# Row jobs first, taps as sums and differences, and two pieces of work moved across stage borders

## The chip, the core and the metric

One Trainium2 chip, one core. The kernel is one program in which every engine has a list of instructions of its own: TensorE (PE in the profile), VectorE (DVE), ScalarE (ACT), GpSimd (POOL) and SyncE (SP). Engines wait for one another with counted semaphores. The metric is device time in microseconds. All arithmetic is 32-bit float; one matmul call of the program stands in the trace as two MATMUL records, a transposition as one.

## The reference, cut to what matters

Two layers over 1024 latent and 128 context tokens of width 1024. Each layer mixes tokens and then runs a routed mixture of 16 experts.

```python
hs = rms_norm(xs, norm1_g[l]) * (1.0 + sc1s) + sh1s        # the same for the context tokens
# layer 0 (even):
proj = hs @ w_in                                            # hyena input 1536 | q | k | v | g, 512 each
h = (sin_features @ f3w).reshape(L, 2, 2, 512) * window     # two filters, each forward and backward
h = h / (sum(abs(h), axis=(0, 2)) + EPS)
kern = concatenate([fwd, 0, bwd[1:][::-1]])                 # per filter
z = long_conv(v, kern[0], hbias[0]) * x1                    # v, x1, x2 from the hyena input
y_hy = long_conv(z, kern[1], hbias[1]) * x2
y_ret = silu(g) * head_group_norm(retention(q, k, v))       # chunks of 128, forward and backward
y = concatenate([y_hy, y_ret]) @ w_out
# layer 1 (odd): q, k, v = split(hs @ w_in, 3); rotary on q and k; differential attention; output projection
xs = xs + gate * y                                          # then norm, router, top-k, experts, residual
```

Outputs: both token sets after a final norm, the context's retention state, and its keys and values.

## The kernel before, in words

**Tiles and weights.** The 1152 tokens are nine tiles of 128 (0 to 7 latent, 8 context). Every weight matrix is cut into units of 2 MB (1024 rows by 512 columns, or tables of that size). SP loads units in one fixed order into `ring`, which has four slots; a unit is loaded when the unit four before it has been given back. Four big tensors hold everything else and are reused by each stage: `big`, `hT`, `yT`, `misc`. Each stage names views of them. PSUM (`ps`) has eight banks of 512 columns.

**The order of work** is written out by hand for each engine. The stages are: start (filters of the convolution, and modulation vectors from 24 weight units), normalization `n10`, the combined projection of the even layer, retention, convolution, output projection, normalization `n20`, experts; then `n11`, the projection of the odd layer, attention, output projection, `n21`, experts.

**Start.** A list `start_plan` mixes three kinds of step on PE, ACT and DVE. A *tap* step makes 512 filter columns for a tile of positions and one direction: PE multiplies `f3w` by the features, DVE multiplies by the window into `FH` (L1667), ACT takes the absolute value (L1330), DVE adds it to `facc`. After both directions of a tile, DVE makes their sum and difference into `FS`. There are 18 tap steps per filter, with a modulation unit after every third. A *sum* step adds up `facc` across partitions on PE (L810); DVE adds EPS (L1679) and inverts. Then *dft* steps transform `FS`, and POOL writes the spectra to memory.

**Normalization.** POOL loads the tiles of X. For three tiles at a time ACT squares and sums each tile (L1353), DVE and ACT make the inverse root, and DVE scales the tiles into `XN` (L1725). PE turns each tile (eight 128 by 128 transpositions, L838); ACT writes four of the turned blocks to `hT` with scale and shift (L1346) and DVE the other four. All nine tiles are turned before the first projection matmul.

**Projection.** A *T job* (column job, L856) computes 128 output columns for all tokens, transposed: 8 steps in depth times 3 groups of 384 tokens, 48 records. An *N job* (row job, L859) computes 512 columns for one tile of tokens: 16 records. Jobs alternate between two groups of three banks; ACT evacuates each, and job j waits for the evacuation of job j - 2. The even layer runs 8 T jobs (q, k), 18 N jobs (v, g) and 12 T jobs (hyena); the hyena columns go through a short convolution on DVE and out to memory (`ud`). The odd layer runs 16 T jobs (q, k) and 18 N jobs (v).

**Retention to convolution.** After the last chunk product on PE (L914), `r.o` lets POOL load `ud` back into `zT` (two loads of four pieces). PE turns the gated retention result of nine tiles into the upper half of `yT` (the depth blocks 4 to 7 of the output projection). The convolution has eight items: item i is filter i // 4, channel block i % 4. For an item PE turns the piece (`turn`, L949), ACT copies it to `vt` (L1418), PE transforms it (`forward`, L966, 64 records, and two products for the context), ACT copies the upper half of the spectrum and the context part, DVE reads the spectrum out of PSUM (L1889, L1890), DVE and POOL multiply with the filter, PE transforms back (`back`, L992), ACT copies (L1439), and DVE forms bias and gate. POOL starts each item with six short operations for the context and goes on with four main ones. PE runs two items ahead: `turn` and `forward` of i + 2 stand before `back` of i.

**Output projection.** PE first spreads the gate over partitions (32 records, L1022), which ACT copies into `grow`. Then 18 jobs of 16 records (tile and half, L1034) use four banks in turn, and DVE adds gate times result to X.

Of the kernel before, what the change touches and what calls it, by code (L numbers as in the profile page):

```python
# [17 lines left out]
ALU = mybir.AluOpType  # L18
# [6 lines left out]
P = 128  # L25
# [84 lines left out]
def build(nc, a, out, tab):  # L110

    with ExitStack() as ctx:
        def sb(name, shape, dt=F32):
# [11 lines left out]
                "o.g": 1, "o.gev": 4, "o.mm": 2 * T, "o.x": 2 * T, "o.x_out": 16 * 8, "o.xn_out": 16 * 8,  # L125
# [14 lines left out]
                   "a.ckT": ("r.ktev", T), "a.tev": ("r.oev", T), "a.e": ("h.vtev", 24), "h.xt": ("f.h3", 36), "h.cx": ("f.abs", 36), "h.cs": ("f.acc", 36),  # L140
                   "h.Y": ("f.taps", 36), "h.uw": ("f.dftmm", 18), "h.yc": ("f.sum", 2), "h.xh": ("f.fold", 2),
                   "h.cxev": ("p.u", 12), "h.ycev": ("f.arg", 2), "h.yev": ("f.sin", 2),
# [74 lines left out]
        even_units = w_units(a["w_in_even"][0], [1536, 2048, 2560, 3072, 0, 512, 1024])  # L217
# [15 lines left out]
        odd_units = w_units(a["w_in_odd"][0], range(0, 3072, 512))  # L233
# [22 lines left out]
        FH = big[:, 0:9216].rearrange("p (t d c) -> p t d c", t=T, d=2)  # L256
# [13 lines left out]
        ftmp = big[:, 5120:7168].rearrange("p (f c) -> p f c", f=4)  # L270
        f3w = misc[0:64, :]
        habs = [big[:, 9216 + 512 * i:9728 + 512 * i] for i in range(2)]
# [4 lines left out]
        vtok = big[:, 9216:13824].rearrange("p (t c) -> p t c", t=T)  # L277
        gtok = big[:, 13824:18432].rearrange("p (t c) -> p t c", t=T)
# [19 lines left out]
        vt = big[:, 13824:18432].rearrange("p (b n) -> p b n", b=4)  # L298
# [78 lines left out]
        for o in range(2):  # L377
# [12 lines left out]
        even_jobs = ([(even_units[0], "T", c) for c in range(4)] + [(even_units[1], "T", c) for c in range(4)]  # L390
                     + [(even_units[2], "N", t) for t in range(T)] + [(even_units[3], "N", t) for t in range(T)]
                     + [(even_units[4 + c // 4], "T", c % 4) for c in range(12)])
        odd_jobs = ([(odd_units[c // 4], "T", c % 4) for c in range(16)]
                    + [(odd_units[4 + u], "N", t) for u in range(2) for t in range(T)])
# [102 lines left out]
        def _(pool):  # L497
# [19 lines left out]
            for o in range(2):  # L517
                if o == 1:

                    pool.wait_ge(*at("f.fold", 2))  # L520
                    load_x(a["x_sample"][0], a["x_prompt"][0], (8, 7))
# [9 lines left out]
                if o == 1:  # L531
                    load_x(a["x_sample"][0], a["x_prompt"][0], (6, 5, 0, 1, 2, 3))
# [25 lines left out]
            for i in range(2):  # L558
                ld(zT[i], ud[4 * i:4 * i + 4].rearrange("c p t -> p c t"), f"h.u{i}")
            ld(kctx, kcd, "h.kctx")  # L560

            def hyena():
# [3 lines left out]
                for i in range(8):  # L566
# [16 lines left out]
                    pool.wait_ge(*at("h.cs", i + 1))  # L583
                    if i < 7:
# [157 lines left out]
        def _(pe):  # L742
# [47 lines left out]
            for kind, o, j in start_plan:  # L790
                if kind == "sine":
                    sine_layer(o)
                elif kind == "tap":
                    if j == 0 and o == 0:
                        pe.wait_ge(*at("f.sin", 2))
                    if j >= 4 or o:
                        pe.wait_ge(*at("f.taps", max(18 * o + j - 3, 18 * o)))
# [9 lines left out]
                elif kind == "sum":  # L807
                    pe.wait_ge(*at("f.acc", 18 * (o + 1)))
# [36 lines left out]
            def project(p, jobs):  # L845

                for j, (n, kind, c) in enumerate(jobs):
                    landed(pe, n)
                    if j >= 2:
                        pe.wait_ge(*at(p + "ev", j - 1))  # L850
                    b = 3 * (j % 2)
                    w = slot(n).rearrange("p (k n) -> p k n", k=DK)
                    for k in range(DK):
                        if kind == "T":
                            for g in range(3):
                                i = mm(ps[:, b + g, 0:384], w[:, k, c * P:(c + 1) * P],  # L856
                                       hTv[:, k, g * 384:(g + 1) * 384], start=k == 0, stop=k == DK - 1)
                        else:
                            i = mm(ps[:, b, :], hTv[:, k, c * P:(c + 1) * P], w[:, k, :],  # L859
                                   start=k == 0, stop=k == DK - 1)  # L860
                    i.then_inc(s(p + "mm"), 1)
                pe.wait_ge(*at(p + "ev", len(jobs)))

            def retention():
# [31 lines left out]
                for c in range(T):  # L896
# [32 lines left out]
            def hyena():  # L929

                def turn(i):

                    c = i % 4
                    if i < 4:
                        pe.wait_ge(*at("h.u0", 16))
                    else:
                        pe.wait_ge(*at("h.z", i - 3))
                    for u, tiles in enumerate((range(4), range(4, 8), (8,))):
                        if u < 2 and i:
                            pe.wait_ge(*at(("h.ycev", "h.cxev")[u], (max(i - 2, 0), i)[u]))  # L940
                        if u == 2:
                            pe.wait_ge(*at("h.vtev", 3 * i + 1))
                        for m in tiles:
                            if m < 8:
                                t0 = 512 * (m % 2) + m // 2
# [6 lines left out]
                def forward(i):  # L952
# [6 lines left out]
                    if i:  # L959
                        pe.wait_ge(*at("h.xt", i))  # L960
# [1231 lines left out]
```

## Time and profile before

| what | us |
|---|---|
| median of three runs | 3970.93 (3963.55 to 3975.09) |
| the profiled execution | 3972.35 |
| its span | 3970.4 |
| PE busy with matmuls | 3659.8 (92%) |
| PE busy with weight loads (beside matmuls) | 2883.8 (73%) |
| DVE busy | 1724.4 (43%) |
| ACT busy | 800.1 (20%) |
| POOL busy | 412.3 (10%) |

The mean granted clock of PE is 0.957 of full speed. Shares are averages over stages: experts, projections and attention are dense on PE, and the stages between them are not. Where a row has a count (x8), it stands for so many records that follow one another, the first number is the start of the first, the second their busy time together. A row at the edge of a stretch counts only what lies inside it. "PEclk" is the granted clock as a part of 2.4 GHz: 0.50 is 1.2 GHz.

### The profile page before, as it was taken

To read this page: it belongs to the slowest core of one execution; us is meant where nothing else is said; L and a number is where in the kernel's file an instruction comes from. 1 tells how busy PE (TensorE), PEld (TensorE's weight loads), DVE (VectorE), ACT (ScalarE), POOL (GpSimd) and SP (SyncE) were. 2 spreads that over 40 slices of the span, in tenths; PEclk is the share of its full clock that TensorE was granted. 3 is DMA by queue.
4 is the path that set the end of the run, shared out by engine and by line. 5 is a ranking of instruction groups with operands and counts; after the bars stand their busy time and mean duration, and the time that the engine had idled before them with its cause. 6 is when DMAs were issued, how large, how long until landed. Compare 5 with 4: busy or idle time off the path is not lost. (4 is left out here: it accounts for less than half of the span.)

```text
span 3970.4 us, 53619 instructions
## 1 busy us (share of the span) xinstructions
PE 3659.8 (92%) x22408; PEld 2883.8 (73%) x22408; DVE 1724.4 (43%) x4132; ACT 800.1 (20%) x1878; POOL 412.3 (10%) x547
## 2 busy tenths in 40 slices
PE   5987999888797999999989999999989799999996
PEld 2434545577546999999975554878854699999996
DVE  5453002279625444444413220777733544444442
ACT  1013000112112111111121001656632111111112
POOL 0111000009500000000000000111111000000001
PEclk8998999989897999999999999999999799999998
DMA  9661101212323788888880011000023388888886
GB/s 337 208 221 59 43 30 70 84 64 98 149 85 122 273 284 285 284 284 286 281 286 22 21 43 58 17 9 17 9 80 115 119 273 283 283 283 284 283 277 218
DMA packets 281331, 647.67 MB, mean 163 GB/s; under 512 B 9192, under 2 KB 9569, under 8 KB 279362
## 3 DMA queue, kind: packets, MB, share of 16 engines
q1 hardware_dynamic: 244626, 508.66, 35.6%
q0 software_dynamic: 36464, 135.58, 11.1%
q8 instruction: 178, 2.92, 0.3%
q14 instruction: 63, 0.52, 0.0%
HBM read 580.89 MB, written 57.02 MB: 161 GB/s over the span
## 5 line engine op out<-in xcount | busy, mean ns | idle before, releaser
L1153 PE MATMUL ps<-big,ring 128*128 128x144 f32 x8192 | 1031.7, 288 | 4.2 <-DVE big L2040 4.2
L1153 PEld LDWEIGHTS ps<-big,ring 128*128 128x128 f32 x8192 | 1014.6, 191 | 12.9 <-issue 11.6
L856 PE MATMUL ps<-hT,ring 128*128 128x384 f32 x1728 | 561.3, 489 | 5.8 <-issue 5.8
L1179 PE MATMUL ps<-big,ring 128*128 128x144 f32 x4096 | 512.0, 286 | 0.0
L1179 PEld LDWEIGHTS ps<-big,ring 128*128 128x128 f32 x4096 | 505.6, 190 | 0.0
L856 PEld LDWEIGHTS ps<-hT,ring 128*128 128x128 f32 x1728 | 330.3, 191 | 236.2 <-issue 10.1
L2068 DVE TENSOR_TENSOR big<-big,ps 128x144 f32<-128x144 f32 x256 | 77.9, 304 | 502.8 <-ACT big L1504 499.3
L1504 ACT ACTIVATE big<-ps 128x144 f32<-128x144 f32 x256 | 74.3, 290 | 979.8 <-PE ps L1153 979.8
L1034 PE MATMUL ps<-ring,yT 128*128 128x512 f32 x576 | 247.5, 592 | 0.0
L859 PE MATMUL ps<-ring,hT 128*128 128x512 f32 x576 | 247.5, 592 | 0.0
L2108 DVE TENSOR_REDUCE gst<-ps 128x1 f32<-128x1152 f32 x144 | 173.4, 1232 | 150.8 <-PE ps L1233 150.8
L2040 DVE TENSOR_SCALAR big<-ps,amul,modc 128x128 f32<-128x128 f32 x256 | 84.5, 402 | 319.4 <-PE ps L1106 319.2
L859 PEld LDWEIGHTS ps<-ring,hT 128*128 128x128 f32 x576 | 109.7, 190 | 137.1 <-issue 136.6
L1034 PEld LDWEIGHTS ps<-ring,yT 128*128 128x128 f32 x576 | 109.5, 190 | 136.6 <-issue 136.6
L1992 DVE TENSOR_SCALAR_CACHE_REDUCE yT<-big,yT 128x1024 f32<-128x1024 f32 (+1 forms) x240 | 193.9, 808 | 0.0
L1791 DVE TENSOR_SCALAR yT<-yT,colB 128x1152 f32<-128x1152 f32 x12 | 10.6, 880 | 379.9 <-ACT yT L1393 379.9
L1229 PE MATMUL ps<-big,yT 64*128 64x256 f32 x512 | 153.7, 424 | 23.6 <-ACT hT L1560 22.3
L1517 ACT ACTIVATE yT<-ps,modc 128x128 f32<-128x128 f32 x256 | 94.0, 367 | 394.9 <-PE ps L1179 394.9
L1560 ACT ACTIVATE hT<-ps,gst 128x1152 f32<-128x1152 f32 x144 | 160.9, 1122 | 29.9 <-DVE gst L2108 28.3
L1990 DVE TENSOR_SCALAR_CACHE_REDUCE yT<-big,yT 128x128 f32<-128x128 f32 (+6 forms) x210 | 156.1, 743 | 4.3
L1231 PE MATMUL ps<-ring 64*128 64x256 f32 x512 | 153.9, 424 | 0.0
L825 PE MATMUL ps<-big,hT 128*128 128x512 f32 x256 | 116.9, 613 | 19.1 <-DVE hT L1680 19.1
(367 smaller groups left out, 3987.9 us busy)
## 6 DMA issues: line engine op xcount, KB each, us to landing
ring<-in_moe_wg SPq DMA_DIRECT2D x64, 2048.0 KB, 10.2
ring<-in_moe_wu SPq DMA_DIRECT2D x64, 2048.0 KB, 13.4
ring<-in_moe_wd SPq DMA_DIRECT2D x64, 2048.0 KB, 11.4
ring<-in_w_mod SPq DMA_DIRECT2D x24, 2048.0 KB, 11.8
big<-aff_t POOLq DMA_DIRECT2D x30, 512.0 KB, 3.9
ring<-in_w_in_even SPq DMA_DIRECT2D x7, 2048.0 KB, 7.9
ring<-in_w_in_odd SPq DMA_DIRECT2D x6, 2048.0 KB, 10.1
big<-x_res POOLq DMA_DIRECT2D x24, 512.0 KB, 8.0
```

The lines of the kernel that those rows point to most:

```text
L825: i = mm(ps[:, b + half, :], (fwd_c, fwd_s)[f][:, 4 * half + n, kt * P:(kt + 1) * P], FS[:, 4 * half + n, f, :], start=n == 0, stop=n == 3)
L856: i = mm(ps[:, b + g, 0:384], w[:, k, c * P:(c + 1) * P], hTv[:, k, g * 384:(g + 1) * 384], start=k == 0, stop=k == DK - 1)
L859: i = mm(ps[:, b, :], hTv[:, k, c * P:(c + 1) * P], w[:, k, :], start=k == 0, stop=k == DK - 1)
L1034: i = mm(ps[:, j % 4, :], yTv[:, k, t * P:(t + 1) * P], w[:, k, :], start=k == 0, stop=k == DK - 1)
L1153: last_mm = mm(ps[:, 3 + f % 2, g * CAP:(g + 1) * CAP], w[u - n0][:, k, c * P:(c + 1) * P], xsT[b][:, k, :], start=k == 0, stop=k == DK - 1)
L1179: last_mm = mm(ps[:, 3 + d % 2, 0:CAP], w[4 + d // 4][:, k, (d % 4) * P:(d % 4 + 1) * P], hid[:, k, :], start=k == 0, stop=k == DK - 1)
L1229: mm(ps[:, 3 * m, c:c + 256], own, kTa[near, h, c:c + 256], start=True, stop=True, tile_position=(64 * m, 0))
L1231: mm(ps[:, 3 * m + 1, c:c + 256], other, kTs[h % 2][far, c:c + 256], start=True, stop=True, tile_position=(64 - 64 * m, 0))
L1560: A(eb[:, n % 2, m, 0:w], bank(3 * m, 3)[:, 0:w], ACT.Exp, bias=gstf[:, c + 2 + m:c + 3 + m], accum_out=gstf[:, c + 4 + m:c + 5 + m]).then ...
L1990: ch.raised(ts(junk[:, 0:t0], row[:, 0:t0], mine, 0.0, ALU.is_ge, ALU.add, accum_out=cnt[:, t, 0:1]))
L1992: ch.raised(ts(junk[:, t0:LAT], row[:, t0:LAT], mine, 0.0, ALU.is_gt, ALU.add, accum_out=cnt[:, t, 1:2]))
L2108: nc.vector.tensor_reduce(gstf[:, c + 2 + m:c + 3 + m], bank(3 * m, 3)[:, 0:w], AX.X, ALU.max, negate=True).then_inc(s("a.nm"), 1)
```

## The change

1. Row jobs stand first. In the even layer all v and g row jobs, tile by tile in the order in which tiles are normalized, come before the column jobs; in the odd layer the nine row jobs of one half of v do. `norm_project` on PE turns a tile, waits for ACT's and DVE's columns of it, and then runs the row jobs of the tile before it (`per` = 2 or 1). ACT's `norm(rows=...)` does squares and roots of all groups, then for each tile the evacuation of row jobs and its columns; DVE's `norm(early=True)` scales all groups and then writes columns. Turned tiles use four banks (4 to 7) and row jobs the others. Tiles 8, 7, 6 and 5 of X are loaded before the spectra of the second filter.
2. `f3w` is turned into sum and difference of the two directions once, on DVE, so that taps come out as sum and difference straight into `FS`. `add_taps` joins two absolute values by a maximum (|a+b| and |a-b| have max |a|+|b|), scaled alike by the later division; row 0 is mended on one partition by `first_taps`. Four buffers `habs` in place of two.
3. `turn(0)` and `forward(0)` stand before the turning of the retention result; u is loaded as one piece, three pieces and four pieces. POOL's context of item i + 1 stands before its main part of item i.
4. Before `back(6)`, PE runs the upper half of depth (blocks 4 to 7) of the first four output jobs and the gate, one bank at a time; the lower half follows at the start of the output projection.

```diff
-        even_units = w_units(a["w_in_even"][0], [1536, 2048, 2560, 3072, 0, 512, 1024])
+        even_units = w_units(a["w_in_even"][0], [2560, 3072, 1536, 2048, 0, 512, 1024])
-        odd_units = w_units(a["w_in_odd"][0], range(0, 3072, 512))
+        odd_units = w_units(a["w_in_odd"][0], [2048, 0, 512, 1024, 1536, 2560])
...
+        even_jobs = ([(even_units[g], "N", t) for t in sum(at_first, ()) for g in range(2)]
+                     + [(even_units[2], "T", c) for c in range(4)] + [(even_units[3], "T", c) for c in range(4)]
                      + [(even_units[4 + c // 4], "T", c % 4) for c in range(12)])
+        odd_jobs = ([(odd_units[0], "N", t) for t in sum(by_three, ())]
+                    + [(odd_units[1 + c // 4], "T", c % 4) for c in range(16)]
+                    + [(odd_units[5], "N", t) for t in range(T)])
...
-                    load_x(a["x_sample"][0], a["x_prompt"][0], (8, 7))
+                    load_x(a["x_sample"][0], a["x_prompt"][0], (8, 7, 6, 5))
...
-            for i in range(2):
-                ld(zT[i], ud[4 * i:4 * i + 4].rearrange("c p t -> p c t"), f"h.u{i}")
+            ld(zT[0][:, 0, :], ud[0], "h.u0")
+            ld(zT[0][:, 1:4, :], ud[1:4].rearrange("c p t -> p c t"), "h.u0b")
+            ld(zT[1], ud[4:8].rearrange("c p t -> p c t"), "h.u1")
...
+                context(0)
+                for i in range(8):
+                    if i < 7:
+                        context(i + 1)
...
+            def norm_project(p, groups, pj, jobs, per):
+                tiles = sum(groups, ())
+                for j, t in enumerate(tiles):
+                    pe.wait_ge(*at(p + "xn", j + 1))
                     if j >= 2:
+                        pe.wait_ge(*at(p + "evA", j - 1))
+                        pe.wait_ge(*at(p + "evD", j - 1))
+                    for c in range(DK):
+                        i = tr(ps[:, 4 + 2 * (j % 2) + c // 4, (c % 4) * P:(c % 4 + 1) * P],
+                               XN[:, t, c * P:(c + 1) * P], ident[:, :])
...
+                    if j:
+                        pe.wait_ge(*at(p + "evA", j))
+                        pe.wait_ge(*at(p + "evD", j))
+                        for g in range(per):
+                            job(pj, jobs, per * (j - 1) + g)
...
+                turn(0)
+                forward(0)
                 for t in range(T):
                     pe.wait_ge(*at("r.on", t + 1))
+                    if t == 1:
+                        pe.wait_ge(*at("h.cxev", 1))
...
+                    if i == 6:
+                        pe.wait_ge(*at("h.xt", 8))
+                        pe.wait_ge(*at("h.cxev", 8))
+                        for j in range(4):
+                            out_part(0, j, range(4, 8), True, False)
+                            gate_part(0, j)
                     back(i)
...
+                    if k == 0:
+                        columns(range(2))
+                    for j in range(2, T):
+                        rows(j - 2)
+                        columns((j,))
...
+            for o in range(2):
+                fw, bw = (f3w[:, (2 * o + d) * HW:(2 * o + d + 1) * HW] for d in range(2))
+                both = facc[0:64, 0, :]
+                ch(tt(both, fw, bw, ALU.add))
+                ch(tt(bw, fw, bw, ALU.subtract))
+                i = cp(fw, both)
...
+                ch(tt(h0, h0, h1, ALU.max))
+                tt(facc[:, g, :], h0, facc[:, g, :], ALU.add).then_inc(s("f.acc"), 1)
...
-                    tt(FH[:, j // 2, j % 2, :], ps[:, j % 4, :], win[:, j // 2, :], ALU.mult).then_inc(s("f.taps"), 1)
-                    if j:
-                        add_taps(o, j - 1)
-                    if j > 3 and j % 2 == 0:
-                        sum_taps(j // 2 - 1)
+                    tt(FS[:, j // 2, j % 2, :], ps[:, j % 4, :], win[:, j // 2, :], ALU.mult).then_inc(s("f.taps"), 1)
+                    if j % 2 and j > 1:
+                        add_taps(o, j // 2 - 1)
```

## Rows read from the trace of the kernel before

**Rows 1.** table of stretches: start:end, length, PE, PEld, DVE, ACT, POOL, clock, DMA, GB/s

```profile
303.00:342.40 39.40, 11.87 (x73) 10.82 (x73) 19.75 (x59) 25.08 (x59) 9.17 (x17) 0.70 0.44 148
...
872.00:1057.50 185.50, 143.49 (x895) 129.62 (x895) 163.60 (x128) 36.43 (x54) 144.52 (x108) 0.92 0.26 96
...
2059.00:2096.30 37.30, 12.06 (x73) 10.85 (x73) 19.05 (x52) 24.02 (x58) 5.37 (x10) 0.73 0.54 185
```

**Rows 2.** timeline, 200 to 234: start us, us, engine, line, operation, count [idle before <- releaser]

```profile
209.34 2.84 PE L801 MATMUL ps<-misc,yT 64*128 64x512 f32 x6
...
216.14 0.69 DVE L1667 TENSOR_TENSOR big<-ps,yT 128x512 f32<-128x512 f32 x1
...
218.28 1.98 PE L810 MATMUL ps<-hT,gst 128*128 128x512 f32 x4 [2.83 <-DVE hT L1637]
...
221.97 1.22 DVE L1679 TENSOR_SCALAR hT<-ps 128x1024 f32<-128x1024 f32 x1
```

**Rows 3.** timeline of the first normalization, in stretches from 296 to 372

```profile
316.62 1.06 ACT L1353 ACTIVATE big<-big 128x1024 f32<-128x1024 f32 x1 [31.46 <-DMA big<-in_x_sample]
...
322.51 2.79 PE L838 MATMUL ps<-ident_sb,big 128*128 128x128 f32 x12 [21.59 <-DVE big L1725]
...
332.15 8.53 ACT L1346 ACTIVATE hT<-ps,modc,amul 128x128 f32<-128x128 f32 x24
...
333.36 1.09 PE L838 MATMUL ps<-ident_sb,big 128*128 128x128 f32 x8 [1.38 <-DVE big L1725]
...
342.38 9.03 PE L856 MATMUL ps<-hT,ring 128*128 128x384 f32 x22 [2.86 <-issue]
```

**Rows 4.** groups by line, 342 to 778: busy us, mean ns, idle before

```profile
L856 PE MATMUL ps<-hT,ring 128*128 128x384 f32 x960 | 311.7, 488 | 2.9 <-issue 2.9
...
L859 PE MATMUL ps<-ring,hT 128*128 128x512 f32 x288 | 123.8, 593 | 0.0
```

**Rows 5.** three short stretches of 2 us, columns as in the first group

```profile
850.00:852.00 2.00, 0.00 (x0) 0.00 (x0) 1.60 (x10) 0.56 (x2) 0.73 (x2) 0.80 0.87 212
...
864.00:866.00 2.00, 1.36 (x6) 0.96 (x7) 1.97 (x7) 0.60 (x1) 0.00 (x0) 0.50 0.39 160
...
1022.00:1024.00 2.00, 0.00 (x0) 0.00 (x0) 1.97 (x3) 0.00 (x0) 2.00 (x2) 0.50 1.05 387
```

**Rows 6.** DMA issues by line, 100 to 300: KB each, median us to landing

```profile
big<-in_x_sample POOLq DMA_DIRECT2D x1, 512.0 KB, 4.5
```

**Rows 7.** timeline, 840 to 935: end of retention, convolution loop

```profile
847.33 1.06 PE L914 MATMUL ps<-big,yT 128*128 128x128 f32 x8
...
869.28 2.29 PE L949 MATMUL ps<-ident_sb,big 128*128 128x128 f32 x9 [0.69 <-ACT yT L1408]
...
872.04 8.84 PE L966 MATMUL ps<-big,ring 128*128 128x128 f32 x64 [0.47 <-ACT big L1418]
...
882.04 1.22 DVE L1889 TENSOR_TENSOR big<-ps,big 128x1024 f32<-128x1024 f32 x1 [14.62 <-ACT big L1425]
...
885.40 0.68 DVE L1893 TENSOR_TENSOR yT<-big 128x512 f32<-128x512 f32 x1
...
917.64 2.83 DVE L1893 TENSOR_TENSOR yT<-big 128x512 f32<-128x512 f32 x1
```

**Rows 8.** timeline, 1000 to 1085: end of the convolution, output projection

```profile
1020.90 1.22 DVE L1890 TENSOR_TENSOR big<-ps,big 128x1024 f32<-128x1024 f32 x1
...
1032.69 8.54 PE L992 MATMUL ps<-ring,hT 128*128 128x256 f32 x32 [11.88 <-POOL hT L598]
...
1057.61 3.84 PE L1022 MATMUL ps<-ident_sb,modc 128*128 128x128 f32 x32 [3.54 <-DVE yT L1922]
...
1061.28 24.20 PE L1034 MATMUL ps<-ring,yT 128*128 128x512 f32 x56
```

**Rows 9.** timeline, 2030 to 2100: normalization before the odd layer

```profile
2076.42 5.42 PE L838 MATMUL ps<-ident_sb,big 128*128 128x128 f32 x32 [17.75 <-DVE big L1725]
...
2096.29 4.07 PE L856 MATMUL ps<-hT,ring 128*128 128x384 f32 x7 [2.92 <-issue]
```

More of the change, by code:

```diff
@@ L565, in hyena, with context @@
                 tt = nc.gpsimd.tensor_tensor
-                for i in range(8):
+                def context(i):
                     o, c = i // 4, i % 4
@@ new lines, in turn @@
+            def turn(i):
+                c = i % 4
+                if i < 4:
+                    pe.wait_ge(*at("h.u0b" if i else "h.u0", 16))
+                else:
+                    pe.wait_ge(*at("h.z", i - 3))
+                for u, tiles in enumerate((range(4), range(4, 8), (8,))):
+                    if u < 2 and i:
+                        pe.wait_ge(*at(("h.ycev", "h.cxev")[u], (max(i - 2, 0), i)[u]))
+                    if u == 2:
+                        pe.wait_ge(*at("h.vtev", 3 * i + 1))
+                    for m in tiles:
+                        if m < 8:
+                            t0 = 512 * (m % 2) + m // 2
+                            src = zT[0][:, c, t0:t0 + 4 * P - 3:4]
+                        else:
+                            src = zT[0][:, c, LAT:NT]
+                        ins = tr(ps[:, 6 + u % 2, (m % 4) * P:(m % 4 + 1) * P], src, ident[:, :])
+                    ins.then_inc(s("h.vt"), 1)
@@ L998, in give_back @@
                     pe.sem_inc(s(f"slot{n % NS}_free"), 1)
-                turn(0)
-                forward(0)
                 turn(1)
@@ L1014, in hyena, with gate_part, out_part @@
                 pe.wait_ge(*at("h.ycev", 8))
+            def gate_part(l, j, b=7):
+                g, half = j // 2, j % 2
+                if b == 7 and j:
+                    pe.wait_ge(*at(f"o{l}.gev", j))
+                for c in range(4):
+                    i = mm(ps[:, b, c * P:(c + 1) * P], modc[:, l, 16 + 4 * half + c, g:g + 1].to_broadcast([P, P]),
+                           ident[:, :], start=True, stop=True)
+                i.then_inc(s(f"o{l}.g"), 1)
+            def out_part(l, j, ks, first, last):
+                n = (oute_units, outo_units)[l][j % 2]
+                landed(pe, n)
+                w = slot(n).rearrange("p (k n) -> p k n", k=DK)
+                for k in ks:
+                    i = mm(ps[:, j % 4, :], yTv[:, k, (j // 2) * P:(j // 2 + 1) * P], w[:, k, :],
+                           start=first and k == ks[0], stop=last and k == ks[-1])
+                if last:
+                    i.then_inc(s(f"o{l}.mm"), 1)
@@ L1037, in out_project @@
+                for j in range(2 * T):
+                    if j >= 4:
+                        pe.wait_ge(*at(p + "x", j - 3))
+                    out_part(l, j, range(4) if l == 0 and j < 4 else range(DK), l == 1 or j >= 4, True)
                 pe.wait_ge(*at(p + "mm", 2 * T))
@@ L1336, in _, with norm @@
                     A(mrow[o % 2], ps[:, 6, :], ACT.Copy).then_inc(s("mod.rowev"), 1)
[L1337 removed]
+            def norm(p, l, n, x_ready, groups=by_three, rows=None):
                 def columns(js):
@@ new lines, in turned, with spectra @@
+            def turned(i):
+                for u, n in enumerate((512, 512, P)):
+                    act.wait_ge(*at("h.vt", 3 * i + u + 1))
+                    if u == 0 and i >= 6:
+                        act.wait_ge(*at("h.x", i - 3))
+                        act.wait_ge(*at("h.cx", i - 3))
+                    A(vt[i][:, 512 * u:512 * u + n], ps[:, 6 + u % 2, 0:n], ACT.Copy).then_inc(s("h.vtev"), 1)
+            def spectra(i):
+                upper_half(i)
+                context(i)
```

360 lines of the change are left out of this document (179 added, 181 removed).

## The prediction

> **What bounds the kernel now.** I read the page by stage first. PE carries the span: in the expert stages and the projections it is busy all the time, so time can be won only where it stands still. The table of stretches shows three such places: the first normalization (11.87 us of PE work in 39.4), the convolution (143.49 in 185.5, with DVE at 163.60) and the normalization before the odd layer (12.06 in 37.3) [rows 1]. Then the timeline inside each, to see what PE waits for: in the start stage, PE waits for DVE's sum of taps and then for the reciprocal [rows 2]; in the normalization, for X to land, three squares, a root and a scaling [rows 3]; at the end of retention, for gating and then for the first spectrum [rows 7]; at the convolution's end, for DVE's sums, and behind it 18 output jobs run without a gap [rows 8].
>
> **The change part by part.** Durations are those of the profiled execution, 3972.35 us for a span of 3970.4.
>
> *Taps as sums and differences (A).* DVE loses two adds per tile of taps, and two absolute values are joined by one max in place of two accumulations: of six operations of about 0.69 us four remain. While taps run, PE is busy on them and on modulation rows, so nothing is won there. The end is: the last tap leaves PE at 209.34 + 2.84 = 212.18, but PE's sum starts at 218.28, because DVE is behind, its last tap product starting at 216.14 [rows 2]. With four operations DVE keeps up: product 0.69, then max and add for the last two tiles, 4 x 0.69, and some 0.4 of handing over: 216.0, so the sum starts about 2.2 earlier. It takes 1.98; the next DVE operation started at 221.97, 1.7 after the sum's end, since memsets and the last sums stood before it. What replaces them (two half-microsecond operations on one partition) lies under the sum. New start 218.2: 3.8 gained. The fold of the first filter stands alike; 3.2 for it. A = 7.0; bounds: 4 (only the 1.7 of each fold and little else) to 9. The weights' own transformation (six DVE operations of at most 0.69) lies at the very start, before data-bound modulation; if that cover were gone, it would cost 4.
>
> *Rows of the first projection inside the normalization (B).* Tiles 8 to 5 of X now load a whole stage earlier, so the first square no longer waits for X but for the last transform's matmuls, whose output space it overwrites. PE was free at 322.51 - 21.59 = 300.92; from first square to first transposition the chain took 322.51 - 316.62 = 5.9 [rows 3]. First transposition: 306.8 at the latest; I take 306.3. Two tiles at the low clock, 16 x 0.23 (12 took 2.79): 310. Two row jobs of 16 records, 0.43 each (123.8 / 288) [rows 4], are 13.8: 323.8. Tile 8's transpositions, 1.1: 324.9. The third row job needs the first one evacuated, and ACT does that only behind six squares and two roots of tiles that still land at 316.62 as before: six squares of 1.05 and two roots with their handing over of about 0.9 put it at 325, so PE goes on at about 326. From there nothing is late: per tile ACT has 4 x 0.36 of columns and two copies, against 14.9 of PE. Left are 16 row jobs (110.0), 6 tiles' transpositions (6.6) and the 20 column jobs, 311.7 less the 1.9 that their first 22 records lost at low clock (9.03 / 22 = 0.41 against 0.325) [rows 3, 4]: 309.8. End 752.4. Before: 342.38 + 311.7 + 123.8 = 777.9. B = 25. Low bound 12, if each tile's step has a hand-over of 1.4 in the open; high bound 28. The queues passed: POOL issues four loads before the second filter's writes instead of two; they go out while no weight waits. The weights' order changes, but the first two units have long landed.
>
> *First convolution item before the last transpositions of retention (C).* PE stops at 847.33 + 1.06 = 848.4 [rows 7]. A quarter of u is loaded first; a lone load of its size took 4.5 [rows 6]: 852.9. Turning it 2.76 (872.04 - 869.28), forward 8.84 and its context part 0.6 [rows 7]: 865.1. Queued behind on PE are the nine transpositions of retention, and behind the turn on ACT their copies; by then DVE has all of them ready but the last. At 12 in 2.79 four take 0.93 at the low clock and half at the high one; with the copies I take 7 for the nine: 872.1. ACT's upper half, 1.0, then lets DVE begin at 873.1 in place of 882.04: 8.9. Of it I give back 0.4 in the loop. There DVE and POOL slow one another: one DVE operation took 0.68 with POOL idle and 2.83 beside POOL [rows 7]. Since POOL now does context 1 (six short operations) before its first main item, that item starts about 2.6 later and its first operation no longer lies beside DVE's PSUM reads; against this, context 7 leaves the last DVE item. Bounds for that: 2 lost to 2 won. C = 8.5. Load bounds: landed with the issue (+4), or only at 869.3, where the whole of u is known to be there (-16).
>
> The Trainium skill, page SBUF — State Buffer, section Who interferes with whom, says that a DVE instruction with two SBUF inputs and a GpSimd instruction that reads SBUF lock each other out, and one with a single SBUF input doesn't. That speaks against this edit: by it POOL's first operation moves from a free place to a locked one. The 0.68 and 2.83 agree with it; taken at its worst (2.15 given back, nothing won) C would be 6.8.
>
> *Half of four output jobs and the gate inside the convolution (D).* Once DVE has read the last spectrum, 1020.90 + 1.22 = 1022.1, PE does 4 x 8 records of 0.43, 13.8, and 3.84 of gate [rows 8], at first at the low clock, which it had fallen to [rows 5]; I add 1.8: 1041.5. That pushes the seventh inverse, which began at 1032.69; its 32 records took 8.54, of which some 1.4 were low clock, so 7.2: 1048.9. ACT's copy 2.2, the eighth inverse 7.2: 1058.3, and ACT and DVE 3.54 [rows 8]: 1061.9, where the whole-tile output jobs began at 1061.28. So the gate and 32 of 288 records are gone for 0.6: D = 13.8 - 0.6 = 13.2; less 0.3 for DVE waiting for X on its first tile. D = 12.9. Bounds: -3 (all 17.6 at half clock) to 16.
>
> *Odd layer (E).* Here X lands as before, so the first transposition stays at 2076.42; 32 took 5.42, so two tiles are there by 2079.8, and the first row job starts at 2080 instead of a column job at 2096.29 [rows 9]. The same nine row jobs then run there, with seven tiles' transpositions (7.7) between, and no low-clock start (2.0): E = 16.3 - 7.7 + 2.0 = 10.6. Bounds 5 to 12. Nine row jobs remain behind the last key job, 62 us, against rotation and exchange loads that need some 25: still hidden.
>
> Sum 7.0 + 25.0 + 8.5 + 12.9 + 10.6 = 64.0: 3908.3 by the profiled execution. That one is 1.4 above the median of the runs shown, 3970.93, so I forecast 3907.
>
> **The rivals.**
> 1. *The clock stays low in the row steps, and the kernel gets slower.* Place: the 27 row jobs that now alternate with transpositions, 27 x 6.88 = 186 at the high clock, twice that at 1.2 GHz. For: between 864 and 866, where PE alternated transpositions with short waits, it was 68% busy and had 0.50 throughout [rows 5]. Against: there the waits filled a third of the time, here a step has 6.9 or 13.8 of matmul behind 1.1 of transpositions and, by the working above, no wait. All at the low clock: 3907 + 186 = 4093; it decides the sign once over a third of the row work (64 / 186) runs low. The Trainium skill, TensorE: Matmul & The Clock Gate, section A second HAM failure mode: psum-queue depth-cycling, describes such micro-idling between groups; no row here shows it in dense groups.
> 2. *The output halves hold up the tail.* All 17.6 at low clock: the inverse chain ends 15.8 later, D is -2.9, time 3923. For: the clock was 0.50 from 1022 on after PE's pause [rows 5]. Against: the seventh inverse recovered within its own 8.54.
> 3. *ACT's order holds up the row steps.* Copies, columns and squares are one queue; if each of 18 steps leaves 1.4 of columns and copy open: 25 lost, 3932. For: PE has only two banks for jobs. Against: 2.6 of ACT work in 14.9.
> 4. *The first item comes late.* u lands only as all of it did, and nine transpositions stand behind it: C = -7, 3922. For: four loads share 16 engines; against: the queue takes them in order, and 4.5 was a lone load.
> That the moves don't do what they say (taps bounded by PE anyway) is in A's low bound: 3 us.
>
> **How the numbers follow.** Forecast 0.78, own range 3898 to 3918; rival 1 0.03, rival 2 0.07, rival 3 0.06, rival 4 0.06. With each term at its better end (9 + 28 + 11 + 15 + 12 = 75) the time is 3896, and the runs shown spread by 6 either way of their middle, so the low end is 3894; the high end takes in rivals 2 and 4: 3926. A measurement of this kernel can't tell less than 0.3%, 12 us, from no change. Every case but rival 1 gives more than that: faster 0.94, within 0.03 (rival 3 and 2 together, and half of rival 1), slower 0.03.
>
> **What would show it.** A: PE's sum directly behind its last modulation row. B: first transposition some 5 us after the last transform, one pause before the third row job, none later; column jobs ending near 745 (752 less A). C: DVE's first spectrum operation 9 us sooner after retention's last product than 33.6. D: no idle PE between the eighth forward and the seventh inverse, and 256 records of output jobs in 110 us. E: row jobs within 4 us of the first transposition. Wrong would be: a granted clock under 0.9 in the row phases, a pause in each step, or a convolution loop longer than before.

## The result and the profile after

The changed kernel takes 3901.66 us (median of 4 runs, 3899.31 to 3910.46), before 3970.81: ratio 0.9833 [0.982, 0.9847], 69 us less. Its profiled execution has a span of 3901.4 us and took 3903.96. The forecast of 3907 lies 5 us above the median, and each of the five terms has the forecast sign.

The ends of the stages, read from PE's timeline in both profiles, place the 69.0 us between the spans:

| term, read between | forecast | gained |
|---|---|---|
| A, start of the span to the end of the last modulation row (300.92, 291.78) | 7.0 | 9.1 |
| B, from there to retention's first transposition (778.81, 741.46) | 25.0 | 28.2 |
| C, retention's last product (848.39, 810.87) to DVE's eighth spectrum (1019.65, 975.27) | 8.5 | 6.9 |
| D, from there to the end of the output jobs (1185.04, 1128.77) | 12.9 | 11.9 |
| E, first transposition of the odd layer (2076.42, 2020.13) to attention's first (2470.28, 2402.02) | 10.6 | 12.0 |
| all else (0.2 in retention, 0.7 behind attention's start) | 0 | 0.9 |

The lines on which A, B and C are read: the last modulation row, retention's first transposition and DVE's eighth spectrum, before and then after (retention's last product before is in [rows 7]).

```profile
299.89 1.03 PE L787 MATMUL ps<-small_sb,yT 128*128 128x96 f32 x8
...
778.81 1.09 PE L869 MATMUL ps<-ident_sb,big 128*128 128x128 f32 x8 [1.30 <-ACT yT L1393]
...
1019.65 1.21 DVE L1889 TENSOR_TENSOR big<-ps,big 128x1024 f32<-128x1024 f32 x1
```

```profile
290.75 1.03 PE L794 MATMUL ps<-small_sb,yT 128*128 128x96 f32 x8
...
741.46 0.77 PE L944 MATMUL ps<-ident_sb,big 128*128 128x128 f32 x5 [1.31 <-ACT yT L1457]
...
975.27 1.21 DVE L1996 TENSOR_TENSOR big<-ps,big 128x1024 f32<-128x1024 f32 x1
```

The table of stretches answers [rows 1]. Its columns are start:end, length, busy us (instructions) of PE, PEld, DVE, ACT and POOL, granted clock, DMA share, GB/s. PE fills the normalization now: 130.11 of 130.20 us at clock 1.00 in the even layer's row steps, all of 68.10 in the odd layer's.

```profile
291.80:300.20 8.40, 3.36 (x16) 3.22 (x16) 6.75 (x18) 5.90 (x14) 2.99 (x4) 0.80 0.43 125
300.20:430.40 130.20, 130.11 (x346) 60.66 (x346) 16.23 (x47) 29.14 (x63) 6.38 (x12) 1.00 0.13 44
834.00:1017.20 183.20, 151.06 (x891) 129.92 (x891) 165.72 (x128) 38.37 (x57) 138.35 (x102) 0.95 0.27 97
2003.00:2023.50 20.50, 3.37 (x16) 3.28 (x16) 3.90 (x10) 6.98 (x14) 5.40 (x10) 0.59 0.83 282
2023.50:2091.60 68.10, 68.10 (x202) 33.28 (x201) 15.69 (x42) 22.05 (x53) 0.00 (x0) 1.00 0.04 15
```

The timeline of the second fold (start, us, engine, line, count, idle before) answers [rows 2]: PE's sum waits 1.67 in place of 2.83, and DVE goes on 0.1 after the sum's end in place of 1.7.

```profile
210.17 1.98 PE L818 MATMUL ps<-hT,gst 128*128 128x512 f32 x4 [1.67 <-DVE hT L1738]
...
212.26 1.23 DVE L1778 TENSOR_SCALAR hT<-ps 128x1024 f32<-128x1024 f32 x1 [0.98 <-PE ps L818]
```

PE's timeline of the first row steps answers [rows 3]: the transpositions of two tiles, then two row jobs and the transpositions of one tile in turn, with no idle time in brackets from 300.28 on.

```profile
296.84 3.43 PE L880 MATMUL ps<-ident_sb,big 128*128 128x128 f32 x16 [5.06 <-DVE big L1824]
300.28 13.97 PE L867 MATMUL ps<-ring,hT 128*128 128x512 f32 x32
314.09 1.04 PE L880 MATMUL ps<-ident_sb,big 128*128 128x128 f32 x8
```

The groups by line, 296 to 741, answer [rows 4] and show the row work itself unchanged (593 ns a record in both) and the column work without its start at low clock:

```profile
L864 PE MATMUL ps<-hT,ring 128*128 128x384 f32 x960 | 309.8, 486 | 0.0
L867 PE MATMUL ps<-ring,hT 128*128 128x512 f32 x288 | 125.1, 593 | 0.1
```

The timeline from retention to the first inverse answers [rows 7]. The piece of u is there 4.02 after PE's last product, the transform (L930) ends at 827.05, but ACT copies its upper half only at 834.10, behind nine retention copies. DVE starts 24.35 after retention's last product (33.65 before). POOL's first main operation (L595) stands behind a context (L579, six operations up to 850.25) that waited for ACT.

```profile
814.89 2.08 PE L913 MATMUL ps<-ident_sb,big 128*128 128x128 f32 x9 [4.02 <-DMA big<-hy_u]
...
817.43 9.62 PE L930 MATMUL ps<-hT,ring 128*128 128x128 f32 x64 [0.47 <-ACT hT L1489]
...
834.10 1.02 ACT L1501 ACTIVATE big<-ps 128x1024 f32<-128x1024 f32 x1
...
835.22 1.23 DVE L1996 TENSOR_TENSOR big<-ps,big 128x1024 f32<-128x1024 f32 x1 [5.20 <-ACT big L1501]
...
846.71 1.28 POOL L579 TENSOR_TENSOR hT<-hT,misc 128x128 f32<-128x128 f32 x1 [14.60 <-ACT hT L1509]
...
850.25 2.87 POOL L595 TENSOR_TENSOR hT<-big 128x1024 f32<-128x1024 f32 x1
```

PE at the convolution's end answers [rows 8]: output halves (L1071) and gate (L1061) run without a gap up to the seventh inverse, the first eight records at low clock, and 256 records remain.

```profile
977.80 5.40 PE L1071 MATMUL ps<-ring,yT 128*128 128x512 f32 x8 [3.35 <-DVE big L1997]
983.03 1.05 PE L1061 MATMUL ps<-ident_sb,modc 128*128 128x128 f32 x8
...
997.35 7.07 PE L1027 MATMUL ps<-ring,hT 128*128 128x256 f32 x32
...
1006.53 7.14 PE L1027 MATMUL ps<-ring,hT 128*128 128x256 f32 x32 [1.66 <-issue]
1017.22 111.56 PE L1071 MATMUL ps<-ring,yT 128*128 128x512 f32 x256 [3.54 <-DVE yT L2029]
```

The odd layer answers [rows 9]: row jobs 3.4 after the first transposition.

```profile
2020.13 3.64 PE L880 MATMUL ps<-ident_sb,big 128*128 128x128 f32 x16 [17.74 <-DVE big L1824]
2023.57 7.13 PE L867 MATMUL ps<-ring,hT 128*128 128x512 f32 x16
```

### The profile page after: what moved, and what is told of

Same layout as the page of the kernel before. It is cut to its first block and busy times, and to the rows that moved or that the text cites. A ratio compares the mean times of both kernels' runs of the same rounds, so it can differ in the third digit from the quotient of the medians.

```text
span 3901.4 us, 53614 instructions
## 1 busy us (share of the span) xinstructions
PE 3647.6 (93%) x22408; PEld 2875.5 (74%) x22408; DVE 1712.8 (44%) x4106; ACT 802.8 (21%) x1878; POOL 410.2 (11%) x548
## 5 line engine op out<-in xcount | busy, mean ns | idle before, releaser
L1071 PE MATMUL ps<-ring,yT 128*128 128x512 f32 x576 | 251.5, 598 | 6.9 <-DVE yT L2029 3.5
L1071 PEld LDWEIGHTS ps<-ring,yT 128*128 128x128 f32 x576 | 110.1, 192 | 144.3 <-issue 136.6
L1328 PE MATMUL ps<-big,hT 128*128 128x128 f32 x1040 | 129.6, 277 | 1.6 <-ACT hT L1651 0.6
```

Source lines behind the costliest of these rows:

```text
L1071: i = mm(ps[:, j % 4, :], yTv[:, k, (j // 2) * P:(j // 2 + 1) * P], w[:, k, :], start=first and k == ks[0], stop=last and k == ks[-1])
L1328: i = mm(ps[:, 7, 0:P], aT[:, t * P:(t + 1) * P], v, start=t == 0, stop=t == nt - 1)
```

## The experiments

All but two are edits of the changed kernel; "+" and "-" are medians against its 3901.66, and stages come from each kernel's profile. No run takes the edits of C, D or E back alone: what these gained is read from their stages in the profiles.

**Late X.** Is B's gain the early load of X, or the row jobs?

```diff
-                    load_x(a["x_sample"][0], a["x_prompt"][0], (8, 7, 6, 5))
+                    load_x(a["x_sample"][0], a["x_prompt"][0], (8, 7))
...
-                    load_x(a["x_sample"][0], a["x_prompt"][0], (0, 1, 2, 3))
+                    load_x(a["x_sample"][0], a["x_prompt"][0], (6, 5, 0, 1, 2, 3))
```

> The changed kernel, but tiles 6 and 5 of X are loaded behind the second filter's spectra again, as before. Theory 1 (B's gain has two halves: X is there a stage earlier, and row jobs fill the normalization): the first square waits for X again. In the changed kernel it began 290.95; here it should begin at about 307.5 (316.62 of before less the 9.1 that the start stage won), the first transposition at 313.4 in place of 296.84, all later stages unchanged: +16.5, 3918. Rival (row jobs alone make B; X is hidden behind them): PE's first transposition late, but made up within the row steps, less than +4, 3905 or below. Rival 2 (no early X needed because tile 8 and 7 go first): no change at all.

Measured: 3915.79, +14.1. ACT's first square waited for X, and PE stood 20.93 before its first transposition:

```profile
312.12 1.06 ACT L1401 ACTIVATE big<-big 128x1024 f32<-128x1024 f32 x1 [30.80 <-DMA big<-in_x_sample]
```

```profile
318.00 3.65 PE L880 MATMUL ps<-ident_sb,big 128*128 128x128 f32 x16 [20.93 <-DVE big L1824]
```

That transposition came 21.2 later, 5.3 of which the start stage had lost already (see the taps below); the other 15.9 were kept to within 0.4 until the end. Theory 1 holds: of B's 28.2, 15.9 are the early load, and 12.3 the row jobs in the normalization, nearly what E, which has no early load, gained (12.0).

**No lag.** What is the one-tile lag worth, and does the clock bear pauses in the row steps?

```diff
-                    if j:
-                        pe.wait_ge(*at(p + "evA", j))
-                        pe.wait_ge(*at(p + "evD", j))
-                        for g in range(per):
-                            job(pj, jobs, per * (j - 1) + g)
+                    pe.wait_ge(*at(p + "evA", j + 1))
+                    pe.wait_ge(*at(p + "evD", j + 1))
+                    for g in range(per):
+                        job(pj, jobs, per * j + g)
...
```

(ACT's and DVE's lists follow the same order.)

> The changed kernel, but each tile's row jobs stand right behind its own transpositions in both layers, so PE waits for ACT's and DVE's columns of that tile in each of the 9 + 9 steps. In the kernel before, PE waited 2.87 from its last transposition to the first projection matmul. Theory 1 (the one-tile lag hides a hand-over, and the clock does not fall in such short pauses): 2.4 to 2.9 in each step, 8 steps more per layer than now: +38 to +46 in all, 3940 to 3948, granted clock near 1.00 in the row steps. Rival (my rival 1: such pauses keep the clock at 0.50): the 27 row jobs take up to 186 more, 4000 to 4130. Rival 2 (ACT is free enough to hide it): less than +10.

Measured: 3936.01, +34.3. Every step shows the hand-over; two steps of PE's timeline in the odd layer, and the clock there:

```profile
2051.82 1.04 PE L880 MATMUL ps<-ident_sb,big 128*128 128x128 f32 x8
2054.36 7.11 PE L867 MATMUL ps<-ring,hT 128*128 128x512 f32 x16 [1.51 <-ACT hT L1390]
2061.30 1.04 PE L880 MATMUL ps<-ident_sb,big 128*128 128x128 f32 x8
```

```profile
2050.00:2110.00 60.00, 50.73 (x157) 24.90 (x155) 10.27 (x28) 13.03 (x33) 0.00 (x0) 1.00 0.00 0
```

A step takes 9.48 in place of 7.74 there, and 16.35 in place of 14.61 in the even layer; the stages lengthen by 16.4 and 17.6. Theory 1's mechanism holds at a smaller size: I took 2.4 to 2.9 a step from 2.87, and a step is 1.74 longer. My rival 1 falls: with a pause of 1.5 in every step, 50.73 busy of 60.00, the clock is 1.00, and so it is from 318 to 430 in the even layer. The Trainium skill, TensorE: Matmul & The Clock Gate, section A second HAM failure mode: psum-queue depth-cycling, tells of micro-idling between groups of matmuls that makes the clock swing between its two levels; pauses of 1.5 between groups of 7 to 14 do not do it here.

**POOL's context at its own item.** Why did C win 9.3 at DVE's first spectrum and only 6.9 at the eighth?

```diff
-                context(0)
                 for i in range(8):
-                    if i < 7:
-                        context(i + 1)
+                    context(i)
```

> The changed kernel, but POOL does the context of item i right before its own main part of item i again, as in the kernel before, all else as changed. In the changed kernel C won 9.3 up to DVE's first spectrum and only 6.9 at the eighth; POOL's first main operation waited for the context of item 1 (850.25, where item 0 was ready at 847.67). Theory 1 (context one item ahead costs the difference): POOL's first main operation starts 2.6 earlier, the first inverse some 3 to 5 earlier than 863.92, DVE's last spectrum 2.4 earlier: 3899. Rival (the loop's length is set by the sum of locked work of DVE and POOL, so the order changes nothing, and the last item gets its context back): within 1 of the changed kernel at the eighth spectrum, and up to 3 later at the output projection, 3901 to 3905.

Measured: 3913.88, +12.2, so both theories missed the time. Up to the eighth spectrum theory 1 was right: from retention's last product, POOL's first main operation came 37.19 later (39.38 in the changed kernel) and the eighth spectrum 162.03 (164.40), 2.4 earlier. Then PE lost 11.7 in the output halves, which with the gate took 31.29 up to the seventh inverse in place of 19.55. The second piece of gate stood behind ACT's copy of the first:

```profile
986.06 3.60 PE L1069 MATMUL ps<-ring,yT 128*128 128x512 f32 x8
998.38 2.08 PE L1059 MATMUL ps<-ident_sb,modc 128*128 128x128 f32 x8 [8.72 <-ACT misc L1554]
```

ACT copies the gate into `misc`, where the context's filter spectra lie, so it waits (`h.cs`, 8) until POOL has done the last context, which now follows the seventh main part. So POOL's order, which costs C 2.4, is what lets D run.

**ACT's upper half first.**

```diff
+                    if t == 1:
+                        upper_half(0)
...
-                upper_half(0)
                 turned(1)
```

> The changed kernel, but ACT copies the upper half of item 0's spectrum behind the second of the nine retention copies instead of behind all nine. In the changed kernel the forward transform ended at 827.05, ACT's copy began only at 834.10 and DVE's first spectrum operation at 835.22, though DVE was free from 830.0. Theory 1 (ACT's order, not PE, holds the first item): DVE begins at about 830.4, 4.8 earlier; the second item is then held by its own transform, which ends some 1 to 2 earlier, so the end of the loop moves by 1 to 3: 3899. Rival (DVE and POOL together set the length of the loop whenever it starts): all 4.8 are kept, 3897. Rival 2 (the nine copies, pushed back by 1.0, delay PE's turn of item 1): nothing gained or +1.

Measured: 3902.05, no difference. DVE began 19.35 after retention's last product, 5.0 earlier; POOL's first main operation 37.56, and the eighth spectrum 162.63, both 1.8 earlier, as theory 1 has it. Rival 2's delay is there too, but small: PE's turn of item 1 began 24.01 after that product, 23.38 in the changed kernel. Behind that the first eight output records ran almost wholly at low clock (granted 0.55, 6.67 in place of 5.40), and the output jobs ended only 0.5 earlier, counted from retention's last product. Nothing of that can be seen in the time: from attention's start to the end of the span the same code differs by up to 7 between these profiles (1493 to 1500), so the time does not tell theory 1 from rival 2; the trace does.

```profile
975.65 6.67 PE L1071 MATMUL ps<-ring,yT 128*128 128x512 f32 x8 [3.35 <-DVE big L1998]
```

**The gate where PE stood still.** What does D still pay?

```diff
+                    if i == 5:
+                        pe.wait_ge(*at("h.cxev", 8))
+                        gate_part(0, 0)
                     if i == 6:
+                        gate_part(0, 1)
                         pe.wait_ge(*at("h.xt", 8))
-                        pe.wait_ge(*at("h.cxev", 8))
                         for j in range(4):
                             out_part(0, j, range(4, 8), True, False)
-                            gate_part(0, j)
                     back(i)
+                    if i == 7:
+                        gate_part(0, 2)
+                        pe.wait_ge(*at("h.ycev", 8))
+                        gate_part(0, 3, 6)
...
```

(ACT copies each piece in that order, and only the last two wait for the last context; DVE awaits them before the context tile.)

> The changed kernel, but the four gate pieces of PE go where PE stood still: the first before the sixth inverse (2.1 idle there), the second behind it (3.35 idle before the output halves), the third and fourth behind the eighth inverse (3.5 idle before the output jobs); the rows for the context tile are awaited only there. Theory 1 (in D the gate, 4 x 0.89 = 3.6, and the low clock after 3.35 of idleness, 1.8, stand in the serial stretch, and 1.5 of low clock after it): the seventh inverse begins 5.4 earlier than 997.35 less the eighth spectrum's shift, the output jobs 5 to 7 earlier, 3895 to 3897. Rival (DVE's last sums bound the eighth inverse): the seventh earlier, the eighth not, output jobs at most 1.5 earlier, 3900. Rival 2 (PE's clock is low there whatever stands before): 3.6, 3898.

Measured: 3899.14 (3892.32 to 3903.68), -2.5. PE's timeline:

```profile
974.48 1.05 PE L1067 MATMUL ps<-ident_sb,modc 128*128 128x128 f32 x8
977.99 14.00 PE L1077 MATMUL ps<-ring,yT 128*128 128x512 f32 x32 [2.46 <-DVE big L2009]
...
992.27 7.07 PE L1027 MATMUL ps<-ring,hT 128*128 128x256 f32 x32
...
1001.49 7.14 PE L1027 MATMUL ps<-ring,hT 128*128 128x256 f32 x32 [1.70 <-ACT big L1543]
```

After 2.46 of idleness the 32 records ran at full clock (14.00). The seventh inverse began 5.3 earlier from the eighth spectrum, the output jobs ended 6.6 earlier: theory 1. Only 2.5 of it stands in the median, within the scatter of the two sets of runs; the profiled run was the fastest, and another 5 that its span is shorter lie behind attention's start (1493.9 to the end, 1499.4 in the changed kernel), within the scatter of those stages.

**Taps alone, and before once more.** The other way round: the kernel before with part A only, and the kernel before without any edit.

```diff
-                    tt(FH[:, j // 2, j % 2, :], ps[:, j % 4, :], win[:, j // 2, :], ALU.mult).then_inc(s("f.taps"), 1)
-                    if j:
-                        add_taps(o, j - 1)
-                    if j > 3 and j % 2 == 0:
-                        sum_taps(j // 2 - 1)
+                    tt(FS[:, j // 2, j % 2, :], ps[:, j % 4, :], win[:, j // 2, :], ALU.mult).then_inc(s("f.taps"), 1)
+                    if j % 2 and j > 1:
+                        add_taps(o, j // 2 - 1)
...
```

> The kernel before with the taps' part alone (sums and differences, maximum, four buffers). In the changed kernel the start stage ended 9.14 earlier than in the kernel before, 4.0 of it within the first filter's taps, where PE's clock rose at 43 us in place of 52; two of the four other profiled kernels with the same start code had it rise at about 55 and ended that stage only 3.8 to 4.5 earlier. Theory 1 (A is worth about 4, two folds of 2.5 less some low clock behind them, and the other 5 are when the clock happens to rise): the two folds take 2.5 less each whenever the clock rises; with a late rise the start stage ends near 296.5, with an early one near 291.5; total 3961 to 3967. Rival (the lighter DVE work itself lets the clock rise early, A is worth 9): the early rise in this profile, 3961 or below. Everything behind the start stage as before.

> The kernel before, unchanged, profiled once more, to see whether the end of its start stage has two values too. Theory 1 (the clock's rise at 43 or 52 us is chance): the first filter's sum at 84.6 (late rise) or at about 79.5 (early). Rival (before always rises late): within 0.5 of 84.6.

Measured: taps alone 3967.18 against 3971.98 (ratio 0.9989 [0.998, 0.9998]), 4.8 less, just above theory 1's range and 6 above the rival's. In the second profile of the kernel before, the first filter's sum came at 80.64, in the first at 84.59: two values, as theory 1 has it. The stretch 46 to 52, in the first filter's taps, with the clock third from the right: the kernel before in its first profile and in its second, taps alone, and the changed kernel with late X.

```profile
46.00:52.00 6.00, 6.00 (x20) 2.58 (x23) 3.42 (x6) 1.89 (x3) 0.00 (x0) 0.50 1.05 387
```

```profile
46.00:52.00 6.00, 6.00 (x32) 2.36 (x31) 3.91 (x7) 2.90 (x5) 0.00 (x0) 1.00 1.05 387
```

```profile
46.00:52.00 6.00, 6.00 (x32) 2.33 (x30) 2.71 (x6) 2.68 (x5) 0.00 (x0) 1.00 1.05 387
```

```profile
46.00:52.00 6.00, 6.00 (x17) 2.77 (x19) 2.24 (x4) 1.89 (x3) 0.00 (x0) 0.50 1.05 387
```

The same code has the clock at 0.50 in one execution and at 1.00 in another, before the change as after it. The start stage ended at 300.92 and 296.36 before, at 291.1 to 292.2 in five profiles with the new taps and at 296.4 to 297.1 in three. Early with early, A is 4.2 to 5.3 (4.7 with taps alone); late with late, 3.8 to 4.5; the 9.1 of the table pairs a late one with an early one.

**All three edits.** Gate in the idle places, POOL's context at its own item, ACT's upper half first.

> Three edits on the changed kernel together: the gate in the idle places (as in the run with that alone), POOL's context at its own item, and ACT's upper half behind the second retention copy. Moving the context back cost 9.4 because ACT's gate copies write the space of the context spectra that POOL still read (PE stood 8.72 at the second gate piece); with the gate's rows for latent tiles written over the first filter's part and the others behind the last inverse, that wait is gone. Theory 1: the gains add, 5.4 to 7 from the gate, 2.4 from POOL's order, 2 from ACT's order: 3890 to 3893. Rival (the last sums on DVE, which wait for POOL's last context, become the bound of the eighth inverse): the gate's gain shrinks by 3 to 5, 3894 to 3898. Rival 2 (no more than the gate's gain): 3896.

Measured: 3886.84 (3885.33 to 3889.20, 5 runs), ratio to the kernel before 0.9786 [0.9772, 0.9799]: 14.8 below the changed kernel, the best of all, with runs that don't overlap it, and below what theory 1 and both rivals gave. From retention's last product to the end of the output jobs the profile shows 304.2 in place of 317.9, 13.7 less. POOL's first main operation now waits for DVE's first item and nothing else, and PE for DVE for 0.24 only:

```profile
847.92 2.35 POOL L593 TENSOR_TENSOR hT<-big 128x1024 f32<-128x1024 f32 x1 [10.66 <-DVE big L2027]
```

```profile
975.54 14.00 PE L1075 MATMUL ps<-ring,yT 128*128 128x512 f32 x32 [0.24 <-DVE big L2008]
```

From retention's last product, the eighth spectrum came 157.27 later, 7.1 earlier than in the changed kernel, more than the 2.4 and 1.8 of the two edits alone. From there to the end of the output jobs it took 146.89, as with the gate moved alone (146.87). Five kernels show why the eighth spectrum came so early:

| from retention's last product | DVE's first spectrum | POOL's first main operation | DVE's eighth spectrum | last two apart |
|---|---|---|---|---|
| before | 33.65 | 46.49 | 171.26 | 124.77 |
| changed | 24.35 | 39.38 | 164.40 | 125.02 |
| context at its own item | 24.59 | 37.19 | 162.03 | 124.84 |
| upper half first | 19.35 | 37.56 | 162.63 | 125.07 |
| all three | 19.58 | 32.18 | 157.27 | 125.09 |

POOL's first main operation before, and with the context at its own item:

```profile
894.88 2.36 POOL L588 TENSOR_TENSOR hT<-big 128x1024 f32<-128x1024 f32 x1 [9.95 <-DVE big L1909]
```

```profile
852.57 2.37 POOL L593 TENSOR_TENSOR hT<-big 128x1024 f32<-128x1024 f32 x1 [15.94 <-DVE big L2014]
```

From POOL's first main operation on the loop's length is the same within 0.4 in these kernels (and 124.8 to 125.5 in the other five profiles), while from DVE's first spectrum it is 137.4 to 143.3. Moving the context alone, POOL still waits for DVE's late first item; moving ACT's copy alone, POOL still waits for the second item's context, which needs the second transform; both together free it.

## Why the prediction was right, step by step

Each part won its time in the place that was named. That the sum came out so near is in part luck: A (taken as 4.7, see below), C and D were forecast 2.3, 1.6 and 1.0 too large, B and E 3.2 and 1.4 too small. And about 4.5 of the 69.0 between the two profiles are when the clock rose in the start stage, which differs by as much between two executions of the kernel before; how the other runs divide in that is not known.

**A** was mis-sized. The second fold did as worked out (2.1 up to the sum and 1.6 behind it, 3.7 between the early profiles, forecast 3.8), the first gave 2.4 (from the start of the last taps to the first transform 17.36 in place of 19.75; forecast 3.2), but the first 16 transform records behind each fold took 1.2 and 0.8 longer (9.98 and 9.45 in place of 8.76 and 8.68), since PE's clock rose later in them, a term that the working does not have. The sign that I set, PE's sum directly behind its last modulation row, did not come: it still waited 1.67. So A is 4 to 5, not 7.0; that the pair of profiles shows 9.1 is the clock.

**B** came out 3.2 better. Its own working ends at 25.5, which I took as 25; the rest is mainly that the pause that I placed before the third row job (1.1) did not occur: ACT's first evacuation, from 314.47 to 315.05, ran beside the next tile's transpositions, which PE did until 315.13. The steps took 14.61, not 14.9, since a tile's transpositions (1.04) overlap the jobs and cost only 0.88; and the first transposition came 5.06 after PE's last work of the start stage, not 5.4. Rival 3 (ACT's order) fell: no step waits, in either layer.

**C** failed in one step, "Of it I give back 0.4 in the loop". The first item was right (9.3 won, 8.9 forecast). The give-back is 2.4: POOL's first main operation stands behind the context of item 1, as I had seen ("starts about 2.6 later"), but I let the last item, which context 7 leaves, pay for most of that. It doesn't: the loop counts from POOL's start, and behind the eighth spectrum the two orders cost the same (146.87 with the context ahead, 146.89 with it at its own item, the gate moved in both). My own sign of being wrong, a convolution loop longer than before, did come: from DVE's first spectrum to its eighth 140.05, before 137.61. The 6.8 that I worked out from the lock described in the Trainium skill (SBUF — State Buffer, section Who interferes with whom) is near the measured 6.9, but not by that way: POOL's first main operation took 2.87 beside operations of DVE with both inputs in SBUF and, with the context moved back, 2.37 beside those with one in PSUM. That agrees with the rule, but it is half a microsecond; the rest is the later start. Rival 4 fell: u was there after 4.02, and the nine transpositions with their copies held ACT's upper half for 6.8, forecast 7.

**D** was right in its place and 1.0 off: the halves and the gate took 19.1 together (forecast 19.4), and the whole stretch from the eighth spectrum's end to the whole output jobs 39.5 as against 39.8. What is missing is 1.5 of low clock in the 256 remaining records (111.56 in place of 110.0; the clock is 0.62 from 1017.2 to 1021), which I had not counted: before, the same 3.54 of idleness was followed by full clock (32 gate records in 3.84, then 288 in 123.77). Rival 2 fell; of the halves only the first eight records were slow. The sign of no idle PE between the eighth forward transform and the seventh inverse did not hold as I worded it: PE still stood 2.11 before the sixth inverse and 3.35 until DVE had read the last spectrum, where the working lets the halves begin.

**E** came out 1.4 better: seven transpositions cost 0.88 each, not 1.1. Rival 1 fell in both layers, and the run without lag shows that even a pause of 1.5 in every step would not have brought it about.

## What to carry to other kernels

Where two engines lock each other in a loop, find the one from whose first operation the loop's length is constant, and clear what that one waits for; here an earlier start of the other was worth only what it moved that one (5.0 of DVE gave 1.8). Work moved into a wait costs nothing as far as it fills idle time, so small independent pieces (a gate, a broadcast) go into the shortest gaps, and an order that looks free (a context one item ahead) may be what another piece's buffer depends on. Before a few microseconds between two profiles are called a gain, a second profile of the same code should show what they differ by themselves.

## What the runs showed of the hardware beside this

The clock's rise in the start stage has two outcomes for the same instructions: full before 46 us or only from 52 on, worth about 5 us of 3900; what decides between them, no run here shows. And one idle time has several outcomes too: the same eight output records took 6.67, 5.40 and 3.70 after the same 3.35 of idleness in three kernels (upper half first, changed, late X).
